# Retention's sums of squares: two halves added on GpSimd, one product with ones, placed behind half a projection

## The chip, the cores and the metric

The kernel runs on one NeuronCore of one Trainium2 chip. The metric is the time of one execution on the device in microseconds, lower is better. Before the change the median of 3 runs is 1982.52 us (1979.82 to 1982.61).

## The reference

One decoder layer on 1024 prompt tokens and 32 sample tokens (8 sequences of 4), model width 1024: RMSNorm; a wide input projection that feeds a sliding-window attention and a retention branch; both projected, gated and merged, and an output projection; then RMSNorm and a mixture of 32 expert MLPs (top 1 group, top 2 experts); a final RMSNorm. The change touches retention alone, which has 4 heads with keys of 128 and values of 256:

```
q = rotary(q); k = rotary(k) * dk**-0.5
scores = (q k^T) * decay            # within a chunk of 128 tokens
o = scores v + (q * q_dec) S        # S: state carried from chunk to chunk
S = S * c_dec + (k * k_dec)^T v
o = o * rsqrt(mean(o*o, axis=-1) + 1e-6)   # mean over a head's 256 values
o = o * silu(g)
```

The mean over the 256 values of each token is what the change computes in another way.

## The kernel before, in words

`stage_retention` goes head by head (a loop over three heads and the last one written apart), and in a head tile by tile: t = 0 to 7 are the prompt's chunks of 128 tokens (NB = 8), t = 8 holds the 32 sample tokens; NT = 9. Each engine has its own program; they meet at semaphores. A head's output is held transposed: value index on the partitions, in two halves f = 0, 1 of 128 (DVT = 2), tokens along the free axis.

What a tile passes through:
- `project(t)` (TensorE): q, k, v of the tile, 8 steps of three matmuls (the operands are split in a high and a low part, L152, L153, L154) into bank t % 2. The projection of tile t+2 is done during iteration t, in two halves of 12 matmuls of 128x512.
- ScalarE copies v out (L1225); VectorE multiplies q and k with cos and sin (L1306); GpSimd makes the rotated and the decayed ones of them (L1180, L1181, L1186, L1187), two tiles ahead at most.
- TensorE transposes three of these (L1424) into bank 2, ScalarE copies them to `qkT` (L1232, semaphore `t_out`); TensorE makes the scores (L1434, which waits for `t_out`), VectorE multiplies with the decay (L1316, `s_out`), and TensorE makes the output halves (L1449, L1451) and the state's update (L1453).
- ScalarE squares both output halves into `sq` (L1241, `sq_done`), VectorE multiplies the output with the gate (L1296).
- `sum_squares` (TensorE, L1405): two accumulated products of a 128x128 matrix of ones with the two halves of `sq` give, in bank 6, the sum over 256 values, alike on all partitions (`ss_mm`). VectorE turns it into mean + eps (L1350, `ms_done`), ScalarE takes the root (L1252), VectorE the reciprocal (L1352) and the last product into `ret` (L1355).

The order on TensorE in iteration t is: transposes of t, `sum_squares(t - 1)`, first half of `project(t + 2)`, scores of t, second half of `project(t + 2)`, outputs and state of t. For t = 7 and 8 no projection is left; for t = 8 there is a chunk of the next head's gate in its place (`gate_chunk`, 24 matmuls of 128x352), except in the last head.

The order on ScalarE in iteration t is: copy to `qkT` of t, v of t + 2, (at t = 8 two of the gate's sigmoids), squares of t, at t = 2 and 3 the high part of a next head's weight piece (L1201), then it waits for `ms_done` of t and takes the root. VectorE at t = 2 and 3 makes that piece's low part (L1269) before it comes to L1296 and L1350.

A single fp32 matmul stands in the trace as two records, so the two products of `sum_squares` are four.

Of the kernel before, what the change touches and what calls it, by code (L numbers as in the profile page):

```python
# [24 lines left out]
ALU = mybir.AluOpType  # L25
# [11 lines left out]
NT = NB + 1  # L37
# [8 lines left out]
DVT = DV // P  # L46
# [16 lines left out]
def rows_of(t):  # L63

    return P if t < NB else NS


def apart(eng, ch):


    eng.sem_inc(ch.passed, 1)
# [998 lines left out]
def stage_retention(nc, ch, ret):  # L1070
# [3 lines left out]
    sem = ch.sem  # L1074
# [9 lines left out]
    p_mm, v_out, rot_a, rot_b, rot_done = sem("r_pmm"), sem("r_v"), sem("r_ra"), sem("r_rb"), sem("r_rot")  # L1084
    turned, t_out, s_mm, s_out, o_mm, st_mm, st_out = (
        sem("r_t"), sem("r_tout"), sem("r_smm"), sem("r_sout"), sem("r_omm"), sem("r_stmm"), sem("r_stout"))
    sq_done, ss_mm, ms_done, root_done, rstd_done, og_done, r_done = (
        sem("r_sq"), sem("r_ssmm"), sem("r_ms"), sem("r_root"), sem("r_rstd"), sem("r_og"), sem("r_r"))
    s0_in, s0_new, s0_stored, stored = sem("r_s0"), sem("r_s0n"), ch.s0_stored, ch.s_stored
    km_done, z_mm, dec_done = sem("r_km"), sem("r_zmm"), sem("r_dec")  # L1090
    with ExitStack() as st:
# [9 lines left out]
        ones = sb("r_ones", [P, P])  # L1101
# [7 lines left out]
        sq, og = sb("r_sqv", [P, DVT, P]), sb("r_ogv", [P, DVT, P])  # L1109
# [4 lines left out]
        banks = ch.banks  # L1114
        half = DK // 2

        def out_bank(t, f):

            m = rows_of(t)
            if t == NB:  # L1120
                return banks[4 + 3 * f][:, 0:m]
            return banks[4 + 3 * (t % 2)][:, f * P:f * P + m]
# [10 lines left out]
        with nc.Block() as block:  # L1133
# [19 lines left out]

            @block.gpsimd
            def _(pool):
                pool.wait_ge(tab_in, 16 * 11)
                with pool.Fori(0, RH) as h:
                    pool.wait_ge(rot_done, h * NT)
                    pool.tensor_copy(dec[:, 0:1], qdec[:, ds(h, 1)])
                    pool.tensor_copy(dec[:, 1:2], kdec[:, ds(h, 1)])  # L1160
                    pool.tensor_copy(dec[0:NS, 2:3], sqdec[:, ds(h, 1)]).then_inc(dec_done, 1)
                    pool.wait_ge(s0_stored, h * 16)
                    apart(pool, ch)
                    pool.dma_start(S0[:], ch.state_ret[:, ds(h, 1)].rearrange("b o d e -> d (b o) e")).then_inc(s0_in, 16)
                    for t in range(NT):
                        m = rows_of(t)
                        n = h * NT + t + 1
                        r = rot[0:m, t % 2]
                        a, b = (x[0:m].rearrange("p a (s d) -> p a s d", s=2) for x in (ta, tb))
                        dst = r.rearrange("p (a b) (s d) -> p a b s d", b=2, s=2)[:, :, 0]  # L1170
                        pool.wait_ge(rot_a, n)

                        if t >= 2:
                            pool.wait_ge(turned, n - 2)
                            pool.wait_ge(st_mm, h * NB + t - 1)
                        else:
                            pool.wait_ge(turned, h * NT)
                            pool.wait_ge(st_mm, h * NB)
                            pool.wait_ge(km_done, h * DB)
                        pool.tensor_tensor(dst[:, :, 0], a[:, :, 0], b[:, :, 1], ALU.subtract)  # L1180
                        pool.tensor_tensor(dst[:, :, 1], a[:, :, 1], b[:, :, 0], ALU.add).then_inc(rot_b, 1)  # L1181
                        pool.wait_ge(rot_b, n)
                        pool.wait_ge(dec_done, h + 1)
                        apart(pool, ch)
                        col = 0 if t < NB else 2
                        pool.tensor_scalar(r[:, 1, :], r[:, 0, :], dec[0:m, col:col + 1], None, ALU.mult)  # L1186
                        pool.tensor_scalar(r[:, 3, :], r[:, 2, :], dec[0:m, 1:2], None, ALU.mult).then_inc(rot_done, 1)  # L1187
                    pool.wait_ge(st_out, h * NB + NB)
                    apart(pool, ch)
                    pool.dma_start(ch.new_state_prompt[ds(h, 1)].rearrange("o d e -> d (o e)"), S[:]).then_inc(stored, 16)  # L1190
                    pool.wait_ge(s0_new, h * DB + DB)
                    apart(pool, ch)
                    pool.dma_start(ch.new_state_sample[:, ds(h, 1)].rearrange("b o d e -> d (b o) e"), S0[:]).then_inc(s0_stored, 16)
# [175 lines left out]
            def _(pe):  # L1369
                def body(h, last):  # L1370
# [28 lines left out]

                    def sum_squares(t):  # L1400
                        m = rows_of(t)
                        pe.wait_ge(sq_done, h * NT + t + 1)
                        pe.wait_ge(ms_done, h * NT + t)
                        for f in range(DVT):
                            mm = pe.matmul(banks[6][:, 0:m], ones[:], sq[:, f, 0:m], start=(f == 0), stop=(f == DVT - 1))  # L1405
                        mm.then_inc(ss_mm, 1)

                    pe.wait_ge(lo_done, h * PIECES + PIECES)
                    pe.wait_ge(tab_in, 16 * 11)
# [6 lines left out]
                    for t in range(NT):  # L1416
                        m = rows_of(t)
                        n = h * NT + t + 1
                        pe.wait_ge(rot_done, n)
                        pe.wait_ge(t_out, n - 1)  # L1420
                        if t == NB:
                            apart(pe, ch)
                        for a in range(3):
                            tr = pe.transpose(banks[2][:, a * P:a * P + m], rot[0:m, t % 2, a, :], ch.ident[0:m, 0:m])  # L1424
                        tr.then_inc(turned, 1)
                        if t >= 1:
                            sum_squares(t - 1)
                        if t + 2 < NT:
                            project(t + 2, range(KT // 2))
                        if t == NB and not last:  # L1430
                            gate_chunk(0)
                        pe.wait_ge(t_out, n)
                        pe.wait_ge(s_out, n - 1)
                        pe.matmul(banks[3][0:m, 0:m], qkT[:, 2, 0:m], qkT[:, 0, 0:m], start=True, stop=True).then_inc(s_mm, 1)  # L1434
                        if t + 2 < NT:
                            project(t + 2, range(KT // 2, KT))
                        if t == NB and not last:
                            gate_chunk(1)
                        pe.wait_ge(s_out, n)
                        pe.wait_ge(v_out, n)  # L1440
                        if t >= 2:
                            pe.wait_ge(og_done, n - 2 if t < NB else n - 1)
                            pe.wait_ge(sq_done, n - 2 if t < NB else n - 1)
                        if t < NB:
                            if t:
                                pe.wait_ge(st_out, h * NB + t)
                            for f in range(DVT):
                                cols = slice(f * P, (f + 1) * P)
                                mm = pe.matmul(out_bank(t, f), v[:, t % 3, cols], sT[:], start=True, stop=(t == 0))  # L1449
                                if t:  # L1450
                                    mm = pe.matmul(out_bank(t, f), S[:, cols], qkT[:, 1, :], start=False, stop=True)  # L1451
                            mm.then_inc(o_mm, 1)
                            pe.matmul(banks[5][:, 0:DV], rot[:, t % 2, 3, :], v[:, t % 3], start=True, stop=True).then_inc(st_mm, 1)  # L1453
                        else:
                            pe.wait_ge(s0_in, h * 16 + 16)
                            for f in range(DVT):
                                pe.matmul(out_bank(t, f), v[0:m, t % 3, f * P:(f + 1) * P], sT[0:m, 0:m], start=True, stop=False)
                                for b in range(DB):
                                    mm = pe.matmul(out_bank(t, f)[:, b * DL:(b + 1) * DL], S0[:, b, f * P:(f + 1) * P],
                                                   qkT[:, 1, b * DL:(b + 1) * DL], start=False, stop=(b == DB - 1))  # L1460
                            mm.then_inc(o_mm, 1)
                            pe.wait_ge(st_out, h * NB + NB)
                            for b in range(DB):
                                if b % 2 == 0 and not last:
                                    gate_chunk(2 + b // 2)
                                if b >= 2:
                                    pe.wait_ge(s0_new, h * DB + b - 1)
                                pe.wait_ge(km_done, h * DB + b + 1)
                                pe.matmul(state_bank(b), kmask[:, b % 2], v[0:NS, t % 3], start=True, stop=True).then_inc(z_mm, 1)
# [1279 lines left out]
```

## Time and profile before

| | |
|---|---|
| median of 3 runs | 1982.52 us |
| profiled execution | 1976.41 us |
| its span | 1974.6 us |
| PE busy | 1849.6 us, 94% |
| DVE, ACT, POOL busy | 58%, 43%, 24% |
| mean granted TensorE clock | 0.958 |
| retention | about 672 to 1089 us of the span |

The span is from the first to the last instruction of the profiled execution. PE is TensorE's matmuls, PEld its weight loads, DVE VectorE, ACT ScalarE, POOL GpSimd. A matmul's record is longer than the time it holds the engine, since matmuls overlap: from one start to the next is what it costs. The granted clock is 1.00 at 2.4 GHz and 0.50 at 1.2 GHz.

### The profile page before, as it was taken

To read this page: it belongs to the slowest core of one execution; us is meant where nothing else is said; L and a number is where in the kernel's file an instruction comes from. 1 tells how busy PE (TensorE), PEld (TensorE's weight loads), DVE (VectorE), ACT (ScalarE), POOL (GpSimd) and SP (SyncE) were. 2 spreads that over 40 slices of the span, in tenths; PEclk is the share of its full clock that TensorE was granted. 3 is DMA by queue.
4 is the path that set the end of the run, shared out by engine and by line. 5 is a ranking of instruction groups with operands and counts; after the bars stand their busy time and mean duration, and the time that the engine had idled before them with its cause. 6 is when DMAs were issued, how large, how long until landed. Compare 5 with 4: busy or idle time off the path is not lost. (4 is left out here: it accounts for less than half of the span.)

```text
span 1974.6 us, 29399 instructions
## 1 busy us (share of the span) xinstructions
PE 1849.6 (94%) x10060; PEld 1585.7 (80%) x10060; DVE 1144.9 (58%) x1912; ACT 854.6 (43%) x1522; POOL 471.0 (24%) x454
## 2 busy tenths in 40 slices
PE   6989997999998999999999897996999999999997
PEld 5877885999998878888887796875888888888883
DVE  4257666211111243434334444668999999999995
ACT  4245546211111222222211212435887878878873
POOL 3013322000000121203021101222485533333220
PEclk9989998999998999999897898997999999999998
DMA  6111202222213102021020462327999999999996
GB/s 185 63 45 49 54 22 62 69 85 75 64 61 106 47 25 85 21 66 42 24 65 3 143 203 73 117 90 299 389 391 386 381 388 384 387 388 385 386 359 276
DMA packets 186165, 333.09 MB, mean 169 GB/s; under 512 B 36704, under 2 KB 118144, under 8 KB 185008
## 3 DMA queue, kind: packets, MB, share of 16 engines
q1 hardware_dynamic: 163984, 277.55, 39.2%
q0 software_dynamic: 21296, 53.26, 7.6%
q10 hardware_dynamic: 816, 1.38, 0.4%
q8 instruction: 41, 0.67, 0.1%
q14 instruction: 28, 0.23, 0.0%
HBM read 304.11 MB, written 46.35 MB: 177 GB/s over the span
## 5 line engine op out<-in xcount | busy, mean ns | idle before, releaser
L2412 POOL DMA_INDIRECT y_d<-e_y,e_idxs x32 | 138.8, 4338 | 202.1 <-DVE e_y L2516 175.9
L2487 DVE TENSOR_TENSOR e_Lg<-e_rawg,e_Hg 128x1024 fp32r<-128x1024 f32 x128 | 148.2, 1220 | 6.4 <-ACT e_Hg L2436 6.3
L2487 DVE TENSOR_TENSOR e_Lu<-e_rawu,e_Hu 128x1024 fp32r<-128x1024 f32 x128 | 147.9, 1218 | 0.0
L2487 DVE TENSOR_TENSOR e_Ld<-e_rawd,e_Hd 128x1024 fp32r<-128x1024 f32 x124 | 143.3, 1218 | 0.0
L2436 ACT ACTIVATE e_Hg<-e_rawg 128x1024 fp32r<-128x1024 f32 x128 | 125.0, 1051 | 7.3 <-DMA e_rawg<-in_w_gate 7.3
L152 PE MATMUL bank<-r_wH,xH 128*128 128x512 f32 (+1 forms) x288 | 121.5, 422 | 6.3 <-DVE r_wL L1269 3.6
L2436 ACT ACTIVATE e_Hd<-e_rawd 128x1024 fp32r<-128x1024 f32 x124 | 121.5, 1050 | 0.3 <-DMA e_rawd<-in_w_down 0.2
L2436 ACT ACTIVATE e_Hu<-e_rawu 128x1024 fp32r<-128x1024 f32 x124 | 121.0, 1059 | 0.0
L154 PE MATMUL bank<-r_wH,xL 128*128 128x512 f32 (+1 forms) x288 | 116.0, 403 | 0.0
L153 PE MATMUL bank<-r_wL,xH 128*128 128x512 f32 (+1 forms) x288 | 115.7, 402 | 0.0
L1031 DVE TENSOR_TENSOR b_wL<-raw,b_wH 128x1024 fp32r<-128x1024 f32 x24 | 29.2, 1222 | 147.8 <-ACT b_wH L1004 147.8
L152 PE MATMUL bank<-e_Hg,e_xH 128*128 128x512 f32 x256 | 100.7, 394 | 3.1 <-DVE e_xL L2493 3.1
L152 PE MATMUL bank<-e_Hu,e_xH 128*128 128x512 f32 x256 | 103.0, 402 | 0.0
L154 PE MATMUL bank<-e_Hg,e_xL 128*128 128x512 f32 x256 | 100.5, 393 | 0.0
L153 PE MATMUL bank<-e_Lg,e_xH 128*128 128x512 f32 x256 | 100.4, 392 | 0.0
L154 PE MATMUL bank<-e_Hu,e_xL 128*128 128x512 f32 x256 | 100.3, 392 | 0.0
L153 PE MATMUL bank<-e_Lu,e_xH 128*128 128x512 f32 x256 | 99.9, 390 | 0.0
L152 PE MATMUL bank<-e_Hd,e_hH 128*128 128x512 f32 x248 | 99.2, 400 | 0.0
L154 PE MATMUL bank<-e_Hd,e_hL 128*128 128x512 f32 x248 | 97.0, 391 | 0.0
L153 PE MATMUL bank<-e_Ld,e_hH 128*128 128x512 f32 x248 | 96.9, 391 | 0.0
L1306 DVE TENSOR_TENSOR r_ta<-bank,r_cos 128x256 f32<-128x256 f32 (+1 forms) x36 | 15.2, 423 | 124.7 <-ACT r_vn L1225 124.7
L165 PE MATMUL bank<-xH,b_wH 128*128 128x352 f32 x384 | 84.1, 328 | 3.1 <-DVE b_wL L1031 3.1
(413 smaller groups left out, 4808.4 us busy)
## 6 DMA issues: line engine op xcount, KB each, us to landing
e_rawg<-in_w_gate SPq DMA_DIRECT2D x128, 512.0 KB
e_rawu<-in_w_up SPq DMA_DIRECT2D x128, 512.0 KB
e_rawd<-in_w_down SPq DMA_DIRECT2D x124, 512.0 KB
raw<-in_w_in SPq DMA_DIRECT2D x51, 512.0 KB, 4.0
c_Y<-y_d SPq DMA_DIRECT2D x8, 1024.0 KB, 13.8
gate_t<-b_gr_s POOLq DMA_DIRECT2D x8, 528.0 KB, 3.0
m_t<-b_m_s POOLq DMA_DIRECT2D x8, 528.0 KB
m_gate<-gate_t POOLq DMA_DIRECT2D x8, 528.0 KB, 4.0
```

Of the source, the lines that this page charges most:

```text
L152: pe.matmul(out, lh, rh, start=first, stop=False)
L153: pe.matmul(out, lh, rl, start=False, stop=False)
L154: return pe.matmul(out, ll, rh, start=False, stop=last)
L165: mm = pe.matmul(banks[g][:, 0:TG], w[a][:, k, :], x[b][:, k, g * TG:(g + 1) * TG], start=(k == 0 and n == 0), stop=(k == KT - 1 and n == 2))
L1031: dve.tensor_tensor(wL[:, q], raw[:, q], wH[:, q].bitcast(F32), ALU.subtract).then_inc(lo_done, 1)
L1306: ins = dve.tensor_tensor(dst[0:m].rearrange("p a (s d) -> p (a s) d", s=2), x, tab[0:m, t, :].rearrange("p (a d) -> p a d", a=1).broadcas ...
L2412: pool.indirect_dma_start(out=ch.y_d, out_offset=bass.IndirectOffsetOnAxis(ap=idx[:, e % IDX, 1:2], axis=0), in_=y[:], in_offset=None, bou ...
L2436: act.activation(H[kind][:, q], raw[kind][:, q], ACT.Copy).then_inc(w_hi[kind], 1)
L2487: dve.tensor_tensor(L[kind][:, q], raw[kind][:, q], H[kind][:, q].bitcast(F32), ALU.subtract).then_inc(w_lo[kind], 1)
```

## The change

On GpSimd a new helper `add_squares` adds the second half of `sq` to the first, in place. It waits for `sq_done` and raises a new semaphore, `sq_sum`. It is called for tile t - 2 ahead of the rotation of tile t, and for tiles 7 and 8 after the loop over tiles. `sum_squares` waits for `sq_sum` in place of `sq_done` and is one product with ones of the summed half. On TensorE it stands in iteration t behind the first half of `project(t + 2)` (at t = 8 behind the gate's first chunk), directly ahead of the waits of the scores.

```diff
+    sq_sum = sem("r_sqsum")
...
+                def add_squares(h, t):
+                    m = rows_of(t)
+                    pool.wait_ge(sq_done, h * NT + t + 1)
+                    apart(pool, ch)
+                    pool.tensor_tensor(sq[:, 0, 0:m], sq[:, 0, 0:m], sq[:, 1, 0:m], ALU.add).then_inc(sq_sum, 1)
...
+                        if t >= 2:
+                            add_squares(h, t - 2)
                         pool.wait_ge(rot_a, n)
...
+                    add_squares(h, NT - 2)
+                    add_squares(h, NT - 1)
                     pool.wait_ge(st_out, h * NB + NB)
...
                     def sum_squares(t):
                         m = rows_of(t)
-                        pe.wait_ge(sq_done, h * NT + t + 1)
+                        pe.wait_ge(sq_sum, h * NT + t + 1)
                         pe.wait_ge(ms_done, h * NT + t)
-                        for f in range(DVT):
-                            mm = pe.matmul(banks[6][:, 0:m], ones[:], sq[:, f, 0:m], start=(f == 0), stop=(f == DVT - 1))
-                        mm.then_inc(ss_mm, 1)
+                        pe.matmul(banks[6][:, 0:m], ones[:], sq[:, 0, 0:m], start=True, stop=True).then_inc(ss_mm, 1)
...
                         tr.then_inc(turned, 1)
-                        if t >= 1:
-                            sum_squares(t - 1)
                         if t + 2 < NT:
                             project(t + 2, range(KT // 2))
                         if t == NB and not last:
                             gate_chunk(0)
+                        if t >= 1:
+                            sum_squares(t - 1)
                         pe.wait_ge(t_out, n)
```

`apart` raises a semaphore that nobody waits for.

## Rows read from the trace of the kernel before

**Rows 1.** The page: busy time of each engine, its share and instructions.
```profile
PE 1849.6 (94%) x10060; PEld 1585.7 (80%) x10060; DVE 1144.9 (58%) x1912; ACT 854.6 (43%) x1522; POOL 471.0 (24%) x454
```

**Rows 2.** Busy time by stretch: stretch, length, busy of each engine, clock, DMA.
```profile
core 0: us, PE busy (x) PEld busy (x) DVE busy (x) ACT busy (x) POOL busy (x), PEclk, DMA share, GB/s
...
672.80:1089.00 416.20, 401.26 (x2081) 334.22 (x2080) 168.98 (x418) 91.72 (x226) 87.35 (x160) 0.94 0.13 39
```

**Rows 3.** PE's weight loads waiting in retention: us in total, times, longest.
```profile
PEld bank L1434 <- ACT r_qkT L1232: 9.1, 11, 1.3
```

**Rows 4.** Instructions in order, iteration 2 of head 2: start, length, [idle before].
```profile
799.01 0.46 POOL L1180 TENSOR_TENSOR r_rotd<-r_ta,r_tb 128x128 f32<-128x128 f32 x1 [5.27 <-PE bank L1453]
...
799.04 0.65 PE L1405 MATMUL bank<-r_sqv,r_ones 128*128 128x128 f32 x4
...
799.45 0.47 PE L152 MATMUL bank<-r_wH,xH 128*128 128x512 f32 x1
...
800.14 0.31 ACT L1252 ACTIVATE r_rstdv<-r_rstdv 128x128 f32<-128x128 f32 x1 [1.21 <-DVE r_rstdv L1350]
...
802.31 0.38 PE L1434 MATMUL bank<-r_qkT 128*128 128x128 f32 x2
...
802.45 0.48 PE L152 MATMUL bank<-r_wH,xH 128*128 128x512 f32 x1
```

**Rows 5.** The same, iteration 3 of head 2, behind the split of a weight piece.
```profile
806.97 0.65 PE L1405 MATMUL bank<-r_sqv,r_ones 128*128 128x128 f32 x4
...
807.83 1.23 DVE L1269 TENSOR_TENSOR r_wL<-raw,r_wH 128x1024 fp32r<-128x1024 f32 x1 [0.51 <-ACT r_wH L1201]
808.04 1.49 POOL L1186 TENSOR_SCALAR r_rotd<-r_rotd,r_dec_h 128x128 f32<-128x128 f32 x1 [0.23 <-POOL r_rotd L1181]
...
810.43 0.49 PE L1434 MATMUL bank<-r_qkT 128*128 128x128 f32 x2
...
810.67 0.48 PE L152 MATMUL bank<-r_wH,xH 128*128 128x512 f32 x1
```

**Rows 6.** The same, iteration 7 of head 2, where no projection is left.
```profile
838.67 0.45 ACT L1241 ACTIVATE r_sqv<-bank 128x128 f32<-128x128 f32 x2 [0.44 <-PE bank L1451]
...
839.23 0.65 PE L1405 MATMUL bank<-r_sqv,r_ones 128*128 128x128 f32 x4
...
839.91 0.29 DVE L1350 TENSOR_SCALAR r_rstdv<-bank 128x128 f32<-128x128 f32 x1
...
840.24 0.31 ACT L1252 ACTIVATE r_rstdv<-r_rstdv 128x128 f32<-128x128 f32 x1 [1.13 <-DVE r_rstdv L1350]
...
840.45 0.47 ACT L1232 ACTIVATE r_qkT<-bank 128x384 f32<-128x384 f32 x1
...
840.98 0.49 PE L1434 MATMUL bank<-r_qkT 128*128 128x128 f32 x2 [1.10 <-ACT r_qkT L1232]
```

**Rows 7.** The same, iteration 8: of head 2, then of head 4.
```profile
845.54 0.23 ACT L1232 ACTIVATE r_qkT<-bank 128x96 f32<-128x96 f32 x1
...
848.49 0.32 PE L154 MATMUL bank<-xH,r_wL 128*128 128x352 f32 x1
...
848.74 0.25 PE L1434 MATMUL bank<-r_qkT 128*32 128x32 f32 x2
...
1067.03 1.22 PE L1405 MATMUL bank<-r_sqv,r_ones 128*128 128x128 f32 x4
...
1068.29 0.29 DVE L1350 TENSOR_SCALAR r_rstdv<-bank 128x128 f32<-128x128 f32 x1 [0.73 <-PE bank L1405]
```

**Rows 8.** PE by stretch: length, busy, clock; iteration 7 twice, attention last.
```profile
727.75:731.75 4.00, 1.93 (x13) 0.95 0.02 4
732.09:734.78 2.69, 2.69 (x12) 0.51 0.00 0
839.23:843.23 4.00, 1.93 (x15) 1.00 0.00 0
300.00:304.00 4.00, 2.61 (x20) 1.00 0.00 2
```

## Prediction

> **What bounds the kernel now.** I read the page's busy line first, then the stretch of retention by itself, then what TensorE waits for in it, and last the instructions of single tiles in order of time. The busy line gives PE 94% [rows 1]. The stretch of retention (672.8 to 1089.0 us, 416 us, so 104 us a head) has PE busy for 401.3 of 416.2 us at a mean granted clock of 0.94, POOL for only 87 us [rows 2]. TensorE is the bound of the stage, and what PE does or waits for inside a tile is paid in full. The span after retention starts from its last instruction, so a microsecond there is one at the end.
>
> In the list of waits one line matters. The scores of a tile (L1434) waited 11 times for ScalarE's copy of the turned q and k (L1232), at most 1.3 us [rows 3]. The reader is to see that L1434 is the place where TensorE runs into ScalarE when nothing covers it.
>
> In a middle tile it doesn't: the product with ones (L1405, four records: two halves, each passed twice) starts at 799.04, the first half of the next projection at 799.45, and L1434 at 802.31, with no idle time before it [rows 4]. In between ScalarE has taken the square root of the tile before (L1252, 800.14) and then the copy L1232. Its program has them in that order: iteration t starts only after the root of tile t-1, and the root needs the mean (L1350) that VectorE reads from the product with ones. So there is a round trip **PE ones product -> DVE mean -> ACT root -> ACT copy of q, k -> PE scores**, and the half projection between L1405 and L1434 is its cover.
>
> Tile 7 shows the round trip bare, as no projection is left: L1405 at 839.23, L1350 at 839.91, L1252 at 840.24, L1232 at 840.45 for 0.47, L1434 at 840.98 with 1.10 us of idle time before it [rows 6].
>
> **The change, part by part.**
>
> *One product instead of two.* Of four records two go. The four hold PE for 799.45 - 799.04 = 0.41 us, the two of L1434 for 802.45 - 802.31 = 0.14 us with their weights loaded ahead [rows 4]. Bounds for two records fewer are 0.2 (half of 0.41) and 0.27; I take 0.2. Over 32 full tiles that is 6.5 us if nothing else happened.
>
> *The place of the product.* It now stands after the half projection and directly ahead of `pe.wait_ge(t_out, n)`. Call S the start of its two records. Two 128-wide records end 0.38 after their start (L1434, [rows 4]; I use 0.39). The mean starts 0.04 after the end of the last record (1067.03 + 1.22 = 1068.25, then 1068.29, [rows 7]). From mean to root is 840.24 - 839.91 = 0.33, from root to copy 0.21, the copy 0.47, and from its end (840.92) to L1434 0.06 [rows 6]. So L1434 starts at S + 0.39 + 0.04 + 0.33 + 0.21 + 0.47 + 0.06 = S + 1.50, where PE has only the two records (0.2 us) to do: about 1.3 us idle in every tile.
>
> Tile by tile. The half projection takes 802.31 - 799.45 = 2.86 us. Before, from the end of the transposes to the end of L1434 takes 802.45 - 799.04 = 3.41 us. After: 2.86 + 1.50 + 0.24 (L1434 with its weights not loaded ahead, 810.67 - 810.43, [rows 5]) = 4.60. That is **+1.19 us**. In iterations 3 and 4 of the first three heads VectorE's split of a weight piece (L1269, 1.23 us) already delays the mean, and the stretch is 810.67 - 806.97 = 3.70 [rows 5]; after, the split has 2.86 us of cover, so it is 4.60 again, **+0.90**. Sum over iterations 1 to 6: 12 x 1.19 + 6 x 0.90 for heads 1 to 3, 6 x 1.19 for head 4 (it splits nothing) = 26.8 us.
>
> *The add on GpSimd.* No row shows it; the nearest is POOL's tensor_tensor of 128x128 (L1180), 0.46 us [rows 4]. The upper bound is a POOL instruction beside VectorE's long split, L1186 at 1.49 us [rows 5]; the lower is a free add, 0. I take 0.46, the row of the same operation and shape. In iterations 1 to 6 it is hidden: the squares (L1241) end beside the transposes, the product comes 2.86 us after these, and even 1.49 fits. POOL's queue: the add stands ahead of the rotation of tile t, so that rotation comes 0.46 later, but has some 7 us until its transposes.
> The Trainium skill, "GPSIMD Engine Reference", section 1 (Specifications), says that GpSimd shares its SBUF interfaces with VectorE and is slowed by VectorE's instructions with two SBUF inputs. The 1.49 of [rows 5] agrees with it. By that rule the add would be slow where a split runs beside it, in iterations 3 and 4, where the cover holds, and the sum would not move.
>
> In iteration 7 there is no projection, and the add is bare. Squares end at 838.67 + 0.45 = 839.12 [rows 6]; plus 0.06, 0.46 and 0.06 the product starts at 839.70 instead of 839.23, and L1434 at 839.70 + 1.50 = 841.20 instead of 840.98: +0.2 to +0.3, for four heads 1.0 us. With the add at 1.49 it would be 4 us more.
>
> *Iteration 8, heads 1 to 3.* The product moves behind the gate's chunk. Its last record starts at 848.49, and records there are 0.16 apart; without the four records ahead (0.41) the chunk ends at 848.24 = S. The copy is shorter here, 0.23 [rows 7], so L1434 is at S + 1.26 = 849.50 instead of 848.74: +0.76, for three heads 2.3 us. In head 4 there is no chunk: the product was bare already and has two records fewer at half clock (four took 1.22, [rows 7]), -0.5; the last product of that head -0.4. The last products of the other heads are followed by a wait for weights, no gain.
>
> *The queue behind the adds.* After the loop POOL waits for the sample tile's squares before it stores the prompt's state. The store's reader is the next head's first tile, behind two whole projections: hidden.
>
> *Clock.* The granted clock was 0.51 for the 2.69 us after 732.09, behind two gaps in tile 7; the same gaps in head 2 left it at 1.00 [rows 8]. One fall costs 2.69 x 0.49 = 1.3 us. Iteration 7's gaps grow, and I count one fall more: +1.3.
>
> **Sum**: 26.8 + 1.0 + 2.3 - 0.9 + 1.3 = **+30.5 us**. The profiled execution took 1976.4 us (span 1974.6, 1.8 us around it), so it would be 2006.9. The median shown is 1982.5, 6.1 above that execution, so the median after is 1982.5 + 30.5 = **2013**.
>
> **Rivals.**
>
> *A. The clock falls too.* Each of the 27 new gaps of about 1.3 us could pull it down. For it: [rows 8], 732.09. Against it: the fall came after two gaps close together, and a stretch of 4 us in attention with PE busy for only 2.61 kept 1.00 [rows 8]; between the new gaps lie some 7.5 us of matmuls. Price 27 x 1.3 = 35 us: 2048; with half of them 2030.
> The Trainium skill, "TensorE: Matmul & The Clock Gate", section "A second HAM failure mode: psum-queue depth-cycling", tells of a kernel whose short idles between groups of matmuls made the clock swing between its two levels. By that rule the time would be this rival's.
>
> *B. The wait doesn't bind (the other side).* If ScalarE had the copy done before PE comes to L1434, the edit gives what its arithmetic says: 32 x 0.2 for the prompt's tiles, about 0.5 for the samples', and the 0.29 of the six delayed tiles: -8.7 us, 1974. It decides at a round trip of 0.2 us after S, against 1.50 counted; above about 0.4 us a tile grows. For it speaks only that PE shows no idle time there today; against it that today's cover is exactly the half projection which is taken away, and the bare case in tile 7.
>
> *C. GpSimd becomes late.* If the add waited for something else in POOL's order (it stands in iteration t+2 of its loop), the product would wait in every tile. At 1.49 us an add, and the rotation behind it, POOL would be busy some 5.4 us (0.46, 0.46 and three of 1.49) of a 9 us tile, so this stays off the path except in iteration 7: +4 us, 2017.
>
> *D. The shorter chain.* With VectorE free, the mean and the root could follow faster than in tile 7; 0.3 us less a gap gives -8: 2005.
>
> **Chances.** The forecast's mechanism with its own size 0.79, A 0.12, C 0.03, D 0.03, B 0.03. The range is 2004 (D's end) to 2031 (half of A); it leaves out full A and B. Faster than before by over 0.2% (4 us, about what a measurement of this kernel can tell) 0.02, within 0.01, slower 0.97.
>
> **What would show it.** In the profile after, L1434 should wait for ACT L1232 some 32 times (or the wait shown as L1252 <- L1350 of about 0.4 us each), about 1.3 us each; PE's busy share in retention should fall to some 90%; the stretch should be near 447 us instead of 416; a middle tile's period should grow by 1.2 us. The adds should appear on POOL at 0.46 us each, the records of L1405 fall from 144 to 72, and PE's idle time for POOL should be seen only in iteration 7. The granted clock should stay at 1.00 through iterations 1 to 6. The prediction is wrong if L1434 starts within 0.5 us of the product with ones in the middle tiles, or if the clock falls there.

## The result and the profile after

The changed kernel takes 2006.84 us (median of 4 runs, 2005.50 to 2009.42), beside 1981.17 us for the kernel before (4 runs, 1976.10 to 1982.61): ratio 1.0136, 95% interval [1.0114, 1.0158]. It is slower by 25.7 us. The forecast was 2013 with 2004 to 2031 as its range. (Of all executions below one, of e4, took 2674.44 us at a mean granted clock of 0.644; the ratios compare the others.)

The two profiled executions differ by 30.7 us of span (2005.3 against 1974.6), of which retention holds 29.3: from the scores of its first tile to its last root it took 412.7 us before (675.41 to 1088.09) and 441.9 after (676.60 to 1118.55). The rest, 1.4 us, lies in stages that the change doesn't touch: 1.2 ahead of the first scores and 0.2 behind the last root. The lines move: L1405 is now L1415, L1434 is L1443, L1232 is L1243, L1252 (the root) is L1263, L1350 is L1361, L1424 is L1433, L1269 is L1280, and the squares, L1241, now have the number L1252.

Of the page, and PE by stretch (length, busy, clock, DMA): retention, its ends set where [rows 2] has them (2.6 us ahead of the first scores, 0.9 us behind the start of the last root), then the middle tiles of head 2. They answer to [rows 1, 2].

```profile
PE 1848.0 (92%) x9988; PEld 1580.5 (79%) x9988; DVE 1145.0 (57%) x1912; ACT 854.5 (43%) x1522; POOL 463.2 (23%) x490
```

```profile
673.99:1119.46 445.47, 397.43 (x2009) 0.94 0.12 37
806.00:842.00 36.00, 31.60 (x165) 1.00 0.10 29
```

PE is busy for 89.2% of retention instead of 96.4%, and the stretch is 445.5 us long where 447 was forecast. The granted clock in the middle tiles is 1.00, the upper level (2.4 GHz), new gaps or not.

The weight loads' waits in retention, to be set beside [rows 3], and one of the matmuls' own waits:

```profile
PEld bank L1443 <- ACT r_qkT L1243: 40.5, 32, 1.3
...
PEld bank L1415 <- POOL r_sqv L1161: 2.6, 4, 0.7
...
PE bank L1433 <- POOL r_rotd L1196: 1.9, 1, 1.9
```

All 32 tiles that have a product with ones ahead of their scores wait for ScalarE, 1.27 us on average; before it was 11 tiles. For GpSimd's add PE waits four times, once a head. It waits for GpSimd once more, 1.9 us for the rotation at the start of head 4 (L1433): GpSimd stood there until its store of head 3's sample state had landed, not behind an add. The forecast had PE idle for GpSimd only in iteration 7. In order of time, iteration 2 of head 2, beside [rows 4]:

```profile
808.47 0.48 PE L152 MATMUL bank<-r_wH,xH 128*128 128x512 f32 x1
...
808.62 0.46 POOL L1161 TENSOR_TENSOR r_sqv<-r_sqv 128x128 f32<-128x128 f32 x1 [6.33 <-ACT r_sqv L1252]
...
811.34 0.39 PE L1415 MATMUL bank<-r_sqv,r_ones 128*128 128x128 f32 x2
...
811.76 0.29 DVE L1361 TENSOR_SCALAR r_rstdv<-bank 128x128 f32<-128x128 f32 x1 [2.35 <-PE bank L1415]
812.08 0.31 ACT L1263 ACTIVATE r_rstdv<-r_rstdv 128x128 f32<-128x128 f32 x1 [3.65 <-DVE r_rstdv L1361]
812.30 0.47 ACT L1243 ACTIVATE r_qkT<-bank 128x384 f32<-128x384 f32 x1
812.43 0.95 DVE L1363 RECIPROCAL r_rstdv<-r_rstdv 128x128 f32<-128x128 f32 x1 [0.38 <-ACT r_rstdv L1263]
812.82 0.30 PEld L1443 LDWEIGHTS bank<-r_qkT 128*128 128x128 f32 x2 [1.29 <-ACT r_qkT L1243]
812.82 0.49 PE L1443 MATMUL bank<-r_qkT 128*128 128x128 f32 x2 [1.10 <-ACT r_qkT L1243]
...
813.07 0.47 PE L152 MATMUL bank<-r_wH,xH 128*128 128x512 f32 x1
```

Read it downwards: product, mean, root, copy, scores, each started by the one above. The scores come 1.48 us after the product with ones. The add was over at 809.08, 2.26 us before anything needed it. Iteration 7 of head 2, beside [rows 6]:

```profile
853.11 0.45 ACT L1252 ACTIVATE r_sqv<-bank 128x128 f32<-128x128 f32 x2 [0.44 <-PE bank L1460]
...
853.34 0.49 PE L1433 MATMUL bank<-identity,r_rotd 128*128 128x128 f32 x3
...
853.74 0.46 POOL L1161 TENSOR_TENSOR r_sqv<-r_sqv 128x128 f32<-128x128 f32 x1 [6.26 <-ACT r_sqv L1252]
...
854.25 0.49 PE L1415 MATMUL bank<-r_sqv,r_ones 128*128 128x128 f32 x2 [0.41 <-POOL r_sqv L1161]
...
855.84 0.49 PE L1443 MATMUL bank<-r_qkT 128*128 128x128 f32 x2 [1.10 <-ACT r_qkT L1243]
```

Here the add is bare: from the start of the transposes to the product with ones it was 0.33 us before, and is 0.91 now.

### The profile page after: what moved, and what is told of

Read it like the earlier page. It is cut to its first block and busy times, and to the rows that moved or that the text cites. A ratio compares the mean times of both kernels' runs of the same rounds, so it can differ in the third digit from the quotient of the medians.

```text
span 2005.3 us, 29327 instructions
## 1 busy us (share of the span) xinstructions
PE 1848.0 (92%) x9988; PEld 1580.5 (79%) x9988; DVE 1145.0 (57%) x1912; ACT 854.5 (43%) x1522; POOL 463.2 (23%) x490
## 5 line engine op out<-in xcount | busy, mean ns | idle before, releaser
L165 PE MATMUL bank<-xL,b_wH 128*128 128x352 f32 x384 | 83.6, 326 | 0.0
```

The source lines that it names most:

```text
L165: mm = pe.matmul(banks[g][:, 0:TG], w[a][:, k, :], x[b][:, k, g * TG:(g + 1) * TG], start=(k == 0 and n == 0), stop=(k == KT - 1 and n == 2))
```

## The experiments

The theory: the loss is the round trip from the product with ones over VectorE's mean, ScalarE's root and ScalarE's copy to the scores, which the half projection covered. Rivals: GpSimd's add (its lateness or its pace), and a lower clock. Every kernel's time stands beside the kernel before on the same chip. The table gives, worked out from the starts of the scores in each trace in order of time, the us from one tile's scores to the next.

```
                          head 2: it.1   2    3    4    5    6    7     8     retention, all heads
before                           7.48 7.93 8.12 8.23 8.03 7.90 6.39  7.76    412.7
the change                       8.48 9.04 9.03 9.05 9.03 9.01 6.90  8.44    441.9
e1 old place                     7.90 8.34 8.34 8.35 8.34 8.32 6.80  8.06    419.1
e2 place only                    8.72 9.25 9.27 9.27 9.28 9.25 6.52  8.66    442.9
e6 behind three steps            7.78 8.32 8.33 8.33 8.34 8.32 6.93  8.03    418.0
e5 behind one step               7.24 7.69 8.12 8.22 7.77 7.66 6.80  9.07    412.5
e3 root late                     7.22 7.66 7.68 7.68 7.68 7.66 5.56 10.21    405.3
e4 root late, no change          7.47 7.93 7.93 7.93 7.92 7.90 5.38 10.25    411.2
e8 root late, two products       7.44 7.90 7.89 7.89 7.90 7.87 5.38 10.25    411.1
e9 second add                    8.48 9.04 9.03 9.03 9.04 9.01 7.32  9.99    444.1
e11 orders only                  7.48 7.92 7.93 7.93 7.92 7.90 5.38  7.26    397.5
e7 root and finish late          7.22 7.66 7.68 7.68 7.68 7.66 5.56  6.90    392.2
```

(Retention is here from the first tile's scores to the start of the last root.) In the column of iteration 8 the values up to 8.66 stand at a granted clock of 1.00, those from 9.07 on at 0.81 to 0.83 on average. So iteration 8 tells of the clock as well as of the edit; iterations 1 to 6, all at 1.00, tell of the edit alone.

**e1, the product back in its old place.**

```diff
                         tr.then_inc(turned, 1)
+                        if t >= 1:
+                            sum_squares(t - 1)
                         if t + 2 < NT:
                             project(t + 2, range(KT // 2))
                         if t == NB and not last:
                             gate_chunk(0)
-                        if t >= 1:
-                            sum_squares(t - 1)
```

> The change with its product with ones put back right behind the transposes; the add on GpSimd and the single product stay. Theory (round trip): the half projection is again between the product and the scores, so the scores' wait for ScalarE's copy is gone in iterations 1, 2, 5 and 6. What is left is the add, now bare in every tile: PE waits about 0.6 us for it (as it does in iteration 7 after the change), less 0.17 for two records fewer, so +0.42 in 18 tiles, +0.23 in 6, and some 2.3 us in iterations 7 and 8: about +11 us against the kernel before, 1992, half of the change's loss gone. Rival (GpSimd's add, or its pace, is what costs): the loss stays as large as with the change or grows, about 2007 or more.

1986.42 us beside 1981.95, ratio 1.0026 [1.0012, 1.0041]: four fifths of the loss are gone with the place alone, and the add is still there. Iteration 2 of head 2:

```profile
801.63 0.45 POOL L1161 TENSOR_TENSOR r_sqv<-r_sqv 128x128 f32<-128x128 f32 x1 [5.64 <-ACT r_sqv L1252]
...
802.13 0.49 PE L1415 MATMUL bank<-r_sqv,r_ones 128*128 128x128 f32 x2 [0.41 <-POOL r_sqv L1161]
...
802.99 0.31 ACT L1263 ACTIVATE r_rstdv<-r_rstdv 128x128 f32<-128x128 f32 x1 [1.54 <-DVE r_rstdv L1361]
...
803.20 0.47 ACT L1243 ACTIVATE r_qkT<-bank 128x384 f32<-128x384 f32 x1
...
805.24 0.38 PE L1443 MATMUL bank<-r_qkT 128*128 128x128 f32 x2
```

The product waits for the add, the scores for nobody. A tile takes 8.34, +0.41 as forecast (+0.42). The sum was forecast at +11 and came to +4.5 (+6.4 in retention): iteration 8 takes 8.06 in heads 1 to 3 here, at a granted clock of 1.00, where it took 9.28 and 9.32 before in heads 1 and 3, at 0.82 on average. That gain was not foreseen.

**e2, the place alone.** The same lines moved as in the change, in the kernel before; two products, no GpSimd.

> The kernel before with nothing but the product's place changed: two products, no add, behind the half projection. Theory: the full loss and more, since four records take 0.26 us longer than two until the mean can start: 2.86 + 1.76 + 0.24 = 4.86 a tile against 3.41 (18 tiles) and 3.70 (6 tiles), iteration 8 +1.0 in three heads, iteration 7 nothing: about +36 us, 2017. Rival (GpSimd): without the add there is no loss, 1981.

2011.65 us beside 1981.95, ratio 1.0149 [1.0126, 1.0172]. Without any add the loss is there and a little larger; a tile takes 9.26, 0.23 more than with the change (forecast 0.26). GpSimd is not the cause. The sum was forecast at +36 and is +29.7, since the tiles grew by 1.33 where 1.45 was put, and head 4's iteration 8 and end got 2.2 shorter.

**e6, behind three of four steps, and e5, behind one.** (Below with j = 3 and j = 1.)

```diff
                         if t + 2 < NT:
-                            project(t + 2, range(KT // 2))
-                        if t == NB and not last:
-                            gate_chunk(0)
+                            project(t + 2, range(j))
                         if t >= 1:
                             sum_squares(t - 1)
+                        if t + 2 < NT:
+                            project(t + 2, range(j, KT // 2))
+                        if t == NB and not last:
+                            gate_chunk(0)
```

> The change with the product behind three of the half projection's four steps instead of four, so 0.7 us of matmuls stand between it and the scores (at iteration 8 it stands ahead of the gate's chunk). Theory: the scores start 1.50 us after the product whatever stands between, so a tile takes 2.19 + 1.50 + 0.24 = 3.93 us against 4.60 with the change: +0.52 in 18 tiles, +0.23 in 6, 2.3 us in iterations 7 and 8, about +13 us against before, 1994. Rival (a fixed cost of the add or of the single product): no change against 2007.

> The change with the product behind one of the half projection's four steps; ScalarE's order is as it was. Theory: L1415 starts some 0.8 us after the transposes, the scores' copy is ready 1.5 us after that, the three steps left take 2.1 us, so the wait is gone, and the add is done in time. A tile takes 7.67 + 0.1 (one more change between the two kinds of product) = 7.8 us against 7.93, in iterations 3 and 4 VectorE's split keeps 8.0 to 8.2; iteration 7 +0.4 in four heads: 1 to 3 us under the kernel before, 1979. Rival (with ScalarE's old order the copy is late wherever the product stands): the 8.32 us of the place behind three steps, 1986.

e6: 1986.22 beside 1981.95, ratio 1.0022 [1.0010, 1.0034]. e5: 1979.25 beside 1983.26, ratio 0.9986 [0.9974, 0.9998]. One step behind the product (0.7 us of matmuls) takes 0.7 off the tile, 9.03 to 8.32; three steps take the wait away, 7.68, and the two records fewer show at last: 0.25 under the kernel before. For e6 I had put 8.45 (7.93 + 0.52) and 2.3 us for iterations 7 and 8, which together lost nothing (8.03 in iteration 8 of every head but the last), and so 1994, 8 too high; the direction and the size of one step were right. e5's time is the 1979 that was forecast, but its trace doesn't show where: its retention is only 0.2 us under that of before. What iterations 1 to 6 give (4.4) goes again in iteration 7 (1.6, forecast too) and between heads 1, 2 and 3 (3.3, at a granted clock of 0.90 there where it was 0.93). e5, a middle tile:

```profile
801.29 0.39 PE L1415 MATMUL bank<-r_sqv,r_ones 128*128 128x128 f32 x2
...
801.72 0.29 DVE L1361 TENSOR_SCALAR r_rstdv<-bank 128x128 f32<-128x128 f32 x1 [0.27 <-PE bank L1415]
...
802.04 0.31 ACT L1263 ACTIVATE r_rstdv<-r_rstdv 128x128 f32<-128x128 f32 x1 [1.57 <-DVE r_rstdv L1361]
...
802.26 0.47 ACT L1243 ACTIVATE r_qkT<-bank 128x384 f32<-128x384 f32 x1
...
803.61 0.38 PE L1445 MATMUL bank<-r_qkT 128*128 128x128 f32 x2
```

The trip is as long as ever (802.73 - 801.29 = 1.44 us to the end of the copy), but 0.88 us of work are left when it ends.

**e3, the change with ScalarE's root behind its copy.**

```diff
+                    def root(t):
+                        m = rows_of(t)
+                        act.wait_ge(ms_done, h * NT + t + 1)
+                        act.activation(rstd[:, 0:m], rstd[:, 0:m], ACT.Sqrt).then_inc(root_done, 1)
...
                         act.activation(qkT[:, :, 0:m], ..., ACT.Copy).then_inc(t_out, 1)
+                        if t >= 1:
+                            root(t - 1)
...
-                        act.wait_ge(ms_done, h * NT + t + 1)
-                        act.activation(rstd[:, 0:m], rstd[:, 0:m], ACT.Sqrt).then_inc(root_done, 1)
+                    root(NT - 1)
```

> The change, and on ScalarE the root of tile t-1 now stands behind the copy of q and k of tile t instead of ahead of it. Theory: the copy no longer hangs on the product with ones, L1434 finds it ready, and the two records saved a tile show: 32 x 0.2 + 0.5 + 6 x 0.29 = 8.7 less, 1.0 more for the bare add in iteration 7: about -8 us against before, 1973. Rival 1 (GpSimd or VectorE holds the tile's pace): still slower than before, 1990 to 2007. Rival 2 (PE resumes on something else just behind the copy): between, about 1985 to 1995.

1972.63 us beside 1981.95, ratio 0.9958 [0.9941, 0.9975]. With product, add and place as in the change, and two instructions of another engine in the other order, a loss of 25.7 is a gain of 9.3. Of the copy's wait nothing is left, and the single product makes a tile 0.25 us shorter than before (7.68 against 7.93). A middle tile:

```profile
798.65 0.49 ACT L1248 ACTIVATE r_qkT<-bank 128x384 f32<-128x384 f32 x1 [0.32 <-PE bank L1439]
...
801.24 0.38 PE L1421 MATMUL bank<-r_sqv,r_ones 128*128 128x128 f32 x2
...
801.46 0.39 PE L1449 MATMUL bank<-r_qkT 128*128 128x128 f32 x2
...
801.66 0.29 DVE L1367 TENSOR_SCALAR r_rstdv<-bank 128x128 f32<-128x128 f32 x1 [2.34 <-PE bank L1421]
...
801.98 0.31 ACT L1241 ACTIVATE r_rstdv<-r_rstdv 128x128 f32<-128x128 f32 x1 [2.84 <-DVE r_rstdv L1367]
```

The copy is done 2 us before the product with ones, and the scores follow that in 0.22 us.

**e4, the root late in the kernel before, and e8, e3 with two products and no add.**

> The kernel before with nothing but ScalarE's order changed: the root of tile t-1 behind the copy of q and k of tile t. The half projection covers the copy already, so only the small delays of iterations 3 and 4 go (0.6 us a head in heads 1 to 3). Theory (the order on ScalarE is worth nothing by itself, it is what makes the move free): -1.8 us, 1980. Rival (the order alone is where the gain of the other kernel came from): about -8, 1974.

> The root behind the copy and the product behind the half projection, but two products of the two halves as before and no add on GpSimd. It prices the add and the single product alone, against the kernel with both and the root moved (tile period 7.67 us). Theory: two records more are 0.22 us a tile, 32 tiles, period 7.89, less 0.6 us in iteration 7 of four heads where the add was bare: 4 to 5 us slower than that kernel, about 1977. Rival (the add on GpSimd costs as much as it saves): the same, 1972.

e4: 1981.02 beside 1981.69, ratio 0.9994 [0.9985, 1.0003]: the order alone is worth nothing that can be measured in the time; its tiles take 7.93. Its trace shows two things under that: iteration 7 gets 1.0 us shorter in every head (5.38 against 6.39), which wasn't foreseen, and iteration 8 of heads 1 and 2 longer (10.28 and 10.25), at a granted clock of 0.83. e8: 1974.82 beside 1981.69, ratio 0.9961 [0.9947, 0.9974]; e3's ratio was 0.9958, on another chip. The tiles differ as forecast (7.89 against 7.67) and retention by 5.8 us, but the times don't show it: in ratios the two are alike. What the add and the single product bring is shown by the traces, by the times not.

**e9, a second add.** One more add of the same shape ahead of the first, into a spare tile.

> The change with a second add of the same shape on GpSimd ahead of the first, into a spare tile, so each tile's sum comes 0.42 to 0.46 us later. Theory: hidden in iterations 1 to 6 behind the half projection, bare in iteration 7 only: +0.45 in four heads, about 2 us above the change, 2009, and the tile period of iterations 1 to 6 stays at 9.03 us. Rival (GpSimd's pace is in the tile): +0.45 in 32 tiles, 2021.

The tiles stay at 9.03, iteration 7 grows from 6.90 to 7.32, retention by 2.2 us: as the theory has it, and GpSimd's pace is out. (Iteration 7 gives 1.7 of the 2.2; the rest is a lower clock in head 2's iteration 8, 1.5 more, and a shorter joint between heads 3 and 4, 0.9 less.) The time is 2014.30 beside 1981.69, ratio 1.0165 [1.0144, 1.0186], more than the trace's retention explains; so the change was run again.

> The change itself once more, beside the others of this call, to see how far its time scatters. Its profile gave tiles of 9.03 us; the kernel with a second add gave 2014.3 us where its trace puts retention only 2.1 us longer. Theory (the rest was scatter outside retention): 2006 to 2010 here, retention 457 us.

2006.45 us beside 1983.26, ratio 1.0128 [1.0108, 1.0149]; retention 440.0 us by the table's ends (the 457 that was expected counts the first two projections too, and is 455.9 so counted). The medians of e9 and of this run are 7.9 us apart on two chips, their traced executions 4.3 in span, of which retention holds 4.1. A second add explains 1.7 of it; why the executions of e9 took longer than that stays open.

**e7, both orders: VectorE's reciprocal and last product behind the decay product too, and e11, these two orders without the change.** In e3 PE waits 2.33 us in iteration 7 for VectorE's decay product, behind the reciprocal:

```profile
838.58 0.95 DVE L1369 RECIPROCAL r_rstdv<-r_rstdv 128x128 f32<-128x128 f32 x1 [0.38 <-ACT r_rstdv L1241]
...
840.02 0.28 DVE L1333 TENSOR_TENSOR r_sT<-bank,r_decay 128x128 f32<-128x128 f32 x1
...
840.44 0.79 PE L1464 MATMUL bank<-r_sT,r_vn 128*128 128x128 f32 x2 [2.33 <-DVE r_sT L1333]
```

```diff
+                    def finish(t):
+                        ... # the wait for the root, the reciprocal, the product into ret, as before
...
                         dve.tensor_tensor(sT[0:m, 0:m], ...).then_inc(s_out, 1)
+                        if t >= 1:
+                            finish(t - 1)
```

> The change with ScalarE's root behind the copy, and VectorE's reciprocal and last product of tile t-1 behind the decay product of tile t. In the kernel with the root alone moved, PE still waits 2.33 us in iteration 7 for the decay product, which stands behind the reciprocal, and the granted clock fell there. Theory: the wait shrinks to some 0.4 us, -1.9 in four heads, and the clock holds, -1.3 a head: 10 to 13 us under the kernel with the root alone moved, about 1962. Rival (the reciprocal and product delay the next rotation's inputs instead): no better than 1973.

> The kernel before with only the two orders changed: ScalarE's root behind the copy, VectorE's reciprocal and last product behind the decay product; two products in their old place, no add on GpSimd. Against the kernel with both orders and the change (1957) it prices the change in a kernel where nothing waits for it. Theory: iterations 7 and 8 gain as there (about 12 us in all), the tiles stay at 7.93 us against 7.67, 24 x 0.26 = 6.2 us: about 1964 to 1968. Rival (the change is worth nothing there): 1957.

e7: 1956.85 us beside 1981.69, ratio 0.9868 [0.9849, 0.9886], the fastest of all: 25 us under the kernel before and 50 under the change. It is 15.8 under e3 (on another chip), where 10 to 13 was expected; iteration 8 of head 2 takes 6.90 us at a granted clock of 1.00, in e3 10.21 at 0.83. e11: 1966.64 beside 1983.26, ratio 0.9923 [0.9906, 0.9940], as expected. Iteration 7 of e7, where the decay product no longer stands behind the reciprocal:

```profile
832.74 0.29 DVE L1343 TENSOR_TENSOR r_sT<-bank,r_decay 128x128 f32<-128x128 f32 x1
...
833.16 0.48 PE L1471 MATMUL bank<-r_sT,r_vn 128*128 128x128 f32 x2 [0.46 <-DVE r_sT L1343]
833.18 0.95 DVE L1331 RECIPROCAL r_rstdv<-r_rstdv 128x128 f32<-128x128 f32 x1 [0.15 <-ACT r_rstdv L1241]
```

Between e11 and e7 the intervals are apart: where nothing waits for it, the change itself (one product, the add, the place) is worth 0.5% or so, some 11 us. The traces show half of that: retention is 5.3 us shorter, of which the tiles give 24 x 0.25 = 6 us. Where the other half comes from is not shown, nor why e3 and e8, which differ by the same product and add, are alike in time.

## Why the prediction was right

- *The round trip.* The step S + 1.50 was measured at 1.48 (812.82 - 811.34), and the chain is the one named. e2 and e3 show it from both sides: with the place alone the loss is whole, with the root out of the chain it is a gain.
- *Iterations 1 to 6.* Predicted +26.8, measured +24.4 (5.9 or 6.0 in each of heads 1 to 3, 6.5 in head 4). A plain tile grew by 1.10, not 1.19: the projection's first matmul follows the start of the transposes by 0.25 us (808.22 to 808.47), where the ones product followed after 0.32 (798.72 to 799.04), a term the sum hadn't.
- *Iteration 7.* Predicted +1.0, measured +2.0. The add's own time was right (0.46); the hand-overs were taken at 0.06 each and were 0.18 (853.56 to 853.74, ScalarE to GpSimd) and 0.05 after the add, and the product's weights were no longer loaded ahead.
- *Iteration 8.* Heads 1 to 3 predicted +2.3, measured +2.1. In head 4 I had -0.9 for two records fewer in both its products. From the product to the scores 0.4 was indeed saved (1.65 us against 2.09), but ahead of the product iteration 8 took 1.0 more, at a granted clock of 0.54 on average instead of 0.71 over the iteration, so that it grew by 0.6; at the end 0.4 came back. The joints between heads took 0.6 more, for which I had nothing. 0.5 of it lies ahead of head 4, where PE waited 1.9 us for GpSimd's rotation, while the clock was 0.93 there and not 0.90. In front of that rotation GpSimd waits for a store to land, 6.23 us before, 8.54 in the change and 7.65 in its repeat. In the other traces PE's wait there lies between nothing and 1.8 us, and is 0.7 in e2, which has no add, so it isn't shown to come from the edit. With the joints the parts make 29.3.
- *The clock.* Predicted one fall more, +1.3. There was none: iteration 8 of heads 1 to 3 stands at 0.83, 1.00, 0.83, before at 0.82, 1.00, 0.82, and iterations 1 to 6 kept 1.00 in all heads. Only head 4's iteration 8 was lower, as said above. Rival A did not come true: 24 gaps of 1.3 us between groups of matmuls made no swing. The Trainium skill's "TensorE: Matmul & The Clock Gate", section "A second HAM failure mode: psum-queue depth-cycling", has a kernel in which short idles between groups did make one; in this trace they made none.
- *Rival B* (the wait doesn't bind) is out by the 1.27 us that PE waits in each tile. Its 8.7 us of gain are near what e3 gave (9.3) once the wait was out. In e3's trace iterations 1 to 6 give 7.9 of it; iteration 7 gives 3.3 more, and iteration 8 and the joints take 3.7 back, so the nearness is in part chance.
- *Rivals C and D* (a late GpSimd, a shorter chain) are out: in the middle tiles no wait for the add shows, and with a second add they still take 9.03 (e9); the chain took its 1.48.
- *From execution to median.* The spans differ by 30.7, the prediction said 30.5, and the medians differ by 25.7 (in the repeat by 23.2). That 30.5 and 30.7 agree so well is in part luck: the middle tiles (2.4 less) and the fall of the clock that never came (1.3 less) were put too high, and iteration 7, head 4's end, the joints and the stages outside retention (1.0, 1.1, 0.6 and 1.4 more) too low or at nothing. The sum stood on an execution that was 5 to 6 us under the median of its kernel, so 2013 was some 6 too high. Retention itself took 29.3 longer, in the repeat's trace 27.3. Where the other executions of the kernel before spend the rest can't be seen.

## What to carry to other kernels

Before a product is moved later, follow its result through the *program order* of every engine that reads it: ScalarE's root and ScalarE's copy had no data in common, and still the copy stood behind the root. The work between an instruction and the next wait downstream is the cover. A move spends it one for one; it costs time from where the cover is shorter than the chain (here 2.87 us were moved away and a tile grew by 1.10; of e6's step of 0.7 all showed). It can be had back by moving the first engine's product (e5) or by swapping two instructions on the second (e3). When a bare case of the chain stands in the trace (here iteration 7), its gaps are the price list.

## What was not expected of the hardware

The GpSimd instruction that stands beside VectorE's long split L1280 stretches, and it need not be the same one: before it was L1186 at 1.49 us [rows 5], and with the add ahead of it the rotation's second sum is there instead, at 1.50 us and not 0.46. In the change, iteration 3 of head 2:

```profile
818.45 1.23 DVE L1280 TENSOR_TENSOR r_wL<-raw,r_wH 128x1024 fp32r<-128x1024 f32 x1 [0.51 <-ACT r_wH L1212]
818.49 1.50 POOL L1190 TENSOR_TENSOR r_rotd<-r_ta,r_tb 128x128 f32<-128x128 f32 x1
```

The Trainium skill's "GPSIMD Engine Reference", section 1, has contention between GpSimd and VectorE instructions with two SBUF inputs; the traces agree, and it was off the path each time.

Whether the clock falls behind iteration 7's gaps isn't set by their length alone: in the kernel before the same gaps were followed by 0.51 in head 1 and left 1.00 in head 2 [rows 8]. In e1, with PE waiting for the add there too, iteration 8 kept 1.00 in all of heads 1 to 3. What decides it stays open.
